# A zero product ahead of runs of three-pass products in a two-block transformer kernel

## The reference

```python
x = first_block(x, ...)     # i = 0: attention with 8 heads; i = 1: pooling over 2, 4, 8, 16 tokens;
                            # after each  x + squared_relu_mlp(rms_norm(x), w_up, w_down), d_ff 4096
h = h + merged @ w_o        # second block: a state-space branch and a latent attention of 16 heads
                            # from one wide projection w_in, merged by two gates
h = h + memory_cross_attention(rms_norm_2(h), rms_norm_2(mem), w_xq, w_xkv, w_xo)
h = h + hierarchical_moe(rms_norm_2(h), ...)      # 32 experts, 2 per token
return rms_norm_2(h, norm_final)
```

## Time and profile before

| | |
|---|---|
| runs of the kernel, us | 1225.2 median (1223.16, 1225.2, 1232.94) |
| the profiled execution, us | 1225.7 |
| its span, first to last instruction, us | 1223.7 |
| PE busy, us (share), instructions | 1189.7 (97%), 8980 |
| PE weight loads busy, us (share) | 1000.8 (82%) |
| DVE busy, us (share) | 787.9 (64%) |
| ACT busy, us (share) | 608.5 (50%) |
| mean granted clock of TensorE | 0.997 |

### The profile page before, as it was taken

How to read it: one execution, slowest core, us unless ns; L and a number is a source line. 1 busy time by engine, 2 the same in 40 slices (tenths; PEclk the granted TensorE clock), 3 DMA queues, 4 the chain that set the end, 5 groups by cost and what they waited for, 6 DMA issues and landing times.

```text
span 1223.7 us, 22272 instructions
## 1 busy us (share of the span) xinstructions
PE 1189.7 (97%) x8980; PEld 1000.8 (82%) x8980; DVE 787.9 (64%) x1330; ACT 608.5 (50%) x990; POOL 97.3 (8%) x100
## 2 busy tenths in 40 slices
PE   9999999999999999899999998999999999999997
PEld 7979999999899999898999998899999853333332
DVE  6876655566755556899899979869745462321214
ACT  6765545454645454767655586765554421111112
POOL 0000200000200000000000030001100004233301
PEclk9999999999999999999999999999999999999999
DMA  9654556564465565455544274455552999999996
GB/s 310 199 176 135 184 195 189 192 203 138 150 196 188 191 204 177 129 169 172 158 152 139 79 241 172 138 173 164 181 167 92 395 351 413 418 412 412 412 419 240
DMA packets 158707, 269.99 MB, mean 221 GB/s; under 512 B 17402, under 2 KB 121823, under 8 KB 154526
## 3 DMA queue, kind: packets, MB, share of 16 engines
q1 hardware_dynamic: 147824, 260.53, 60.8%
q0 software_dynamic: 10432, 8.16, 2.3%
q10 hardware_dynamic: 366, 0.12, 0.0%
HBM read 287.89 MB, written 12.58 MB: 246 GB/s over the span
## 4 chain that ended last, share of the span: by engine, by line
PE 76%; DVE 16%; ACT 4%; issue 3%; another core or an unknown queue 0%; DVEq 0%; ACTq 0%
PE psum L896 17%; PE psum L898 17%; PE psum L897 17%; PE psum L1509 11%; PE psum L1535 5%; DVE weights_parts L2196 4%; DVE arena L2599 3%; ACT weights_parts L1606 1%; PE psum L1469 1%; DVE smax L2320 1%; PE psum L1403 1%; PE psum L1520 1%; PE psum L1412 1%; DVE arena L2701 1%; DVE arena L2313 1%
## 5 line engine op out<-in xcount | busy, mean ns | idle before, releaser
L2196 DVE TENSOR_TENSOR weights_parts<-ring,weights_parts 128x1024 fp32r<-128x1024 f32 (+3 forms) x312 | 363.3, 1184 | 139.0 <-ACT weights_parts L1606 138.7
L1606 ACT ACTIVATE weights_parts<-ring 128x1024 fp32r<-128x1024 f32 (+3 forms) x312 | 309.4, 1011 | 149.0 <-PE psum L898 148.5
L896 PE MATMUL psum<-xnorm_parts,weights_parts 128*128 128x256 f32 x852 | 243.1, 285 | 6.6 <-DVE arena L2599 2.5
L897 PE MATMUL psum<-xnorm_parts,weights_parts 128*128 128x256 f32 x852 | 237.4, 279 | 0.0
L898 PE MATMUL psum<-xnorm_parts,weights_parts 128*128 128x256 f32 x852 | 237.4, 279 | 0.0
L896 PE MATMUL psum<-expert_cols,weights_parts 128*128 128x256 f32 (+1 forms) x688 | 193.1, 281 | 3.4 <-DVE expert_cols L2214 2.1
L897 PE MATMUL psum<-expert_cols,weights_parts 128*128 128x256 f32 (+1 forms) x688 | 190.7, 277 | 0.0
L898 PE MATMUL psum<-expert_cols,weights_parts 128*128 128x256 f32 (+1 forms) x688 | 190.7, 277 | 0.0
L896 PE MATMUL psum<-hidden_parts,weights_parts 128*128 128x256 f32 x640 | 179.3, 280 | 3.0 <-DVE hidden_parts L2667 1.7
L897 PE MATMUL psum<-hidden_parts,weights_parts 128*128 128x256 f32 x640 | 177.8, 278 | 0.0
L898 PE MATMUL psum<-hidden_parts,weights_parts 128*128 128x256 f32 x640 | 177.8, 278 | 0.0
(11 more groups left out here) (464 smaller groups left out, 1702.8 us busy)
## 6 DMA issues: line engine op xcount, KB each, us to landing
ring<-in_mlp_w_up SPq DMA_DIRECT2D x32, 1024.0 KB, 5.4
ring<-in_mlp_w_down SPq DMA_DIRECT2D x32, 1024.0 KB, 4.9
ring<-in_w_in SPq DMA_DIRECT2D x30, 1024.0 KB, 5.2
ring<-in_attn_w_qkv SPq DMA_DIRECT2D x12, 1024.0 KB, 6.2
expert_raw<-in_w_exp_gate SPq DMA_DIRECT2D x22, 512.0 KB
expert_raw<-in_w_exp_up SPq DMA_DIRECT2D x22, 512.0 KB
ring<-in_w_exp_down SPq DMA_DIRECT2D x11, 1024.0 KB
expert_raw<-in_w_exp_down SPq DMA_DIRECT2D x9, 1024.0 KB
```

What stands on the lines that cost most here:

```text
L896: pe.matmul(out, lh, rh, start=start, stop=False, **more)
L897: pe.matmul(out, lh, rl, start=False, stop=False, **more)
L1606: ins = act.activation(high, src, ACT.Copy)
L2196: ins = dve.tensor_tensor(low, src, high.bitcast(F32), ALU.subtract)
```

## The change

A helper `zero_product(b, start)` issues one bf16 product of the zero tile with itself, 128 by 128 stationary, 512 columns moving, into bank b. It is called behind the wait for the first half's low part and ahead of the first three-pass product. In `project_split` it opens the bank (start=True), and the chunk's own first product opens its columns again; in `add_down` it adds zeros to bank 4 (start=False). No value of the output changes. The flag is set for: qk 2; wo1 2; down 0 in the MLP's loop, in each of its three turns; up 13; "small" 1; xbc 1 and 5; the first gate chunk of groups 1 to 3; the second gate chunk of group 0; qb 0; mout 1; wo2 1. Over one execution that makes 20 products.

```diff
--- before.py
+++ after.py
@@ -903,10 +903,16 @@
                 pe.wait_ge(s["lo_ready"], shift + (2 * n + half + 1))
                 return high, low
 
-            def project_split(n, b, xn_from=None, shift=0, parts=(xh, xl), head_of=None):
+            def zero_product(b, start):
+
+                pe.matmul(bank(b)[:, 0:512], zeros[:, 0:P], zeros[:, 0:512], start=start, stop=False, skip_group_check=True)
+
+            def project_split(n, b, xn_from=None, shift=0, parts=(xh, xl), head_of=None, zero_first=False):
 
                 for m in range(2):
                     high, low = split_half(n, m, shift)
+                    if zero_first and m == 0:
+                        zero_product(b, True)
                     width = high.shape[2]
                     for k in range(KT):
                         if xn_from is not None and m == 0:
@@ -996,14 +1002,15 @@
                 stage = f"mlp{i}"
                 u, first = FILL[stage, "first"]
 
-                def up(it, n, xn_from=None):
+                def up(it, n, xn_from=None, zero_first=False):
                     b = n % 2
                     pe.wait_ge(made[b], it * 2 + (u[b] + n // 2))
-                    project_split(first + (2 * n - 1 if n else 0), b, xn_from, shift=it * 16, parts=PARTS[2 * i + 1])
-
-                def down(it, n, last=False):
+                    project_split(first + (2 * n - 1 if n else 0), b, xn_from, shift=it * 16, parts=PARTS[2 * i + 1],
+                                  zero_first=zero_first)
+
+                def down(it, n, last=False, zero_first=False):
                     pe.wait_ge(s["hid_ready"], it * 4 + (FC * i + n + 1))
-                    add_down(first + (2 * n + 2 if not last else 2 * n + 1), n % 2, it * 16, last)
+                    add_down(first + (2 * n + 2 if not last else 2 * n + 1), n % 2, it * 16, last, zero_first)
 
                 up(0, 0, XN_NO[2 * i + 1])
                 for b in range(4):
@@ -1012,10 +1019,10 @@
                 with pe.Fori(0, 3) as it:
                     for n in range(1, 5):
                         up(it, n)
-                        down(it, n - 1)
+                        down(it, n - 1, zero_first=(n == 1))
                 folded_sum(2 * i + 1, sq_late)
                 for n in range(13, FC):
-                    up(0, n)
+                    up(0, n, zero_first=(n == 13))
                     down(0, n - 1)
                 down(0, FC - 1, last=True)
 
@@ -1025,12 +1032,14 @@
                 for b in range(4, 8):
                     pe.matmul(bank(b), zeros[:, 0:P], zeros[:, :], start=True, stop=False, skip_group_check=True)
 
-            def add_down(n, buf, shift, last):
+            def add_down(n, buf, shift, last, zero_first=False):
 
                 hh = hid_h[:, buf, :].rearrange("p (k t) -> p k t", k=2)
                 hl = hid_l[:, buf, :].rearrange("p (k t) -> p k t", k=2)
                 for half in range(2):
                     high, low = split_half(n, half, shift)
+                    if zero_first and half == 0:
+                        zero_product(4, False)
                     for mm_ in range(4):
                         m = 4 * half + mm_
                         cc = slice(mm_ * P, (mm_ + 1) * P)
@@ -1071,7 +1080,7 @@
                 if j < 2:
                     project_high_first(j, open_bank("qk", j), j == 0)
                 else:
-                    project_split(j, open_bank("qk", j))
+                    project_split(j, open_bank("qk", j), zero_first=(j == 2))
                 if j == 1:
                     root_row()
                     pe.wait_ge(s["more_rows_in"], 16 * (len(ROWS_A) - 1 + len(ROWS_B)))
@@ -1117,7 +1126,7 @@
             wo1_part(0, [KT - 2, KT - 1])
             wo1_part(1, list(range(KT // 2, KT)))
             for j in (2, 3):
-                project_split(c.ordinal["wo1", j], open_bank("wo1", j))
+                project_split(c.ordinal["wo1", j], open_bank("wo1", j), zero_first=(j == 2))
             mlp(0)
 
 
@@ -1175,10 +1184,11 @@
                     total.then_inc(full[sums_bank], 1)
                 mm.then_inc(s["units_done"], 1)
             for j in (1, 2):
-                project_split(c.ordinal["win", j], open_bank("small", j), parts=PARTS["raw"])
+                project_split(c.ordinal["win", j], open_bank("small", j), parts=PARTS["raw"], zero_first=(j == 1))
 
             for j in range(12):
-                project_split(c.ordinal["win", 4 + j], open_bank("xbc", j), XN_NO[5] if j == 0 else None)
+                project_split(c.ordinal["win", 4 + j], open_bank("xbc", j), XN_NO[5] if j == 0 else None,
+                              zero_first=(j in (1, 5)))
                 if j == 4:
                     norm_sum(6)
                     norm_sum(7, sq[:, 3:5, :])
@@ -1190,8 +1200,8 @@
             def z_chunk(j):
                 project_split(c.ordinal["win", 16 + j], open_bank("z", j))
 
-            def gate_chunk(j):
-                project_split(c.ordinal["win", 24 + j], open_bank("gates", j))
+            def gate_chunk(j, zero_first=False):
+                project_split(c.ordinal["win", 24 + j], open_bank("gates", j), zero_first=zero_first)
 
             for g in range(NG):
                 def decays(q):
@@ -1248,11 +1258,11 @@
                     turn_inputs()
                     z_chunk(2 * g + 1)
                     state()
-                    gate_chunk(2 * g)
+                    gate_chunk(2 * g, zero_first=True)
                     b = open_bank("norm", 9 + g)
                     pe.wait_ge(s["gated_folded"], 2 * g)
                     pe.matmul(bank(b)[:, 0:TOK], ones, sq[:, 0, :], start=True, stop=True).then_inc(full[b], 1)
-                gate_chunk(2 * g + 1)
+                gate_chunk(2 * g + 1, zero_first=(g == 0))
                 wait_made("state", g)
                 pe.wait_ge(s["cs_ready"], g + 1)
                 wait_made("xsn", g, 0)
@@ -1303,6 +1313,8 @@
                     return mm
 
                 pe.wait_ge(s["lo_ready"], 2 * n + 1)
+                if j == 0:
+                    zero_product(b, True)
                 no_rope(0)
                 pe.wait_ge(s["lo_ready"], 2 * n + 2)
                 high, low = turned_columns(n)
@@ -1357,7 +1369,8 @@
             pe.wait_ge(s["kpe_copied"], 16)
             attention(LATENT, scores2, values2, CAUSAL, ssd_out)
             for j in range(4):
-                project_split(c.ordinal["mout", j], open_bank("mout", j), head_of=None if j else lambda k: H1 + 2 * k)
+                project_split(c.ordinal["mout", j], open_bank("mout", j), head_of=None if j else lambda k: H1 + 2 * k,
+                              zero_first=(j == 1))
                 if j == 0:
                     pe.wait_ge(s["mem_in"], 16)
                     for i in range(4):
@@ -1369,7 +1382,7 @@
                         mm.then_inc(full[b], 1)
             for j in range(4):
                 project_split(c.ordinal["wo2", j], open_bank("wo2", j), XN_NO["merged"] if j == 0 else None,
-                              parts=PARTS["merged"])
+                              parts=PARTS["merged"], zero_first=(j == 1))
                 if j == 0:
                     folded_sum(8, sq)
 
```

## The result

The changed kernel takes 1236.07 us (median of 12 runs, 1233.51 to 1238.35). The kernel before, run beside it and counted with its first three runs, takes 1229.33 us (12 runs, 1223.16 to 1233.22). The medians lie 6.7 us apart; the ratio on record, which is not the quotient of the medians, is 1.0045, 95% interval 1.0024 to 1.0065, or 5.5 us. So the changed kernel is slower by about half a per cent, where I had forecast 0.6 us less. Two things moved. The change costs some 6 to 7 us, and the kernel before is about 4 us slower than its first three runs said. Both come from the pace of the two MLP loops, as the experiments show.

A forecast was written before the change was run, and what follows sets the result against it. PE's distance between three-pass product starts, fast or slow, was taken to bound the kernel; +0.83 us of terms less 1.50 for pace kept across sums gave about -0.7, so 1224.6 us from a 1225.2 median, range 1221 to 1231.

The forecast's parts named there:

- Two paces, 113 and 118 ns, set where a run begins: Three-pass products on PE start at a fast or slow distance, some 4.45 ns apart, seemingly fixed where a run begins.
- After zero products comes the fast pace: Claimed from three cases: both MLPs behind clear_sums' four zero products, and the first chunk behind seven more.
- The MLPs' term, +1.92 us: Both MLPs, fast already: eight zero products at 0.24 us each on PE's path, nothing gained.
- the rival given 0.07 for both MLPs: Zero products inside both MLPs leave the slow pace behind them: 16 us more, 1236 to 1241 us, chance 0.07.
- wo1 -0.25, the gates +0.02, qb -0.02: Net us in wo1, gates of groups 1 to 3, and qb: 0.22 price per zero product against slow products turned fast.
- the case of a kept pace: If fast pace survives fp32 sums, second chunks gain too: gates 0.63, qb 0.23, wo2 0.64, together 1.50 us.
- qk, "small", xbc at 0: DVE sets the time there and PE's waits cover the price: 0, or +0.24 us each for five if cover is gone.
- wo2 -0.84, and -0.64 behind the sum: wo2, all PE: 238 slow products turn fast, -0.84 us; another 143 behind the fp32 sum, -0.64 if pace is kept.
- Fp32 sums mostly keep the pace, 9 of 12: Pace before and after fp32 sums counted the same in 9 of 12, so the kept total, -0.7 us, was taken.
- The profiled execution as the kernel's level: Profiled execution, 1225.7 us, expected to go to 1225.0; it stood 0.5 above the median of 1225.2.
- the second rival: Zero products inside MLPs leave slow pace: both MLPs 1236 to 1241 us, chance 0.07; one, about 1230, chance 0.06.
- The rule for the length of a product: The skill's columns / 2.4 + 2.5 ns gives 215.8 for zero products; by it the sum would be price only.

The follow-up runs named there:

- e6: Kernel before plus one bf16 zero product ahead of each of the 8 chunks in the MLPs' loops, each of another width (512 to 128 columns); one run, 1240.63 us.
- e10: Kernel before plus loop zero products, 512 columns at every other chunk and 64, 128, 192, 256 or 384 between, entered slow; one run, 1240.96 us.
- e12: Kernel before plus loop zero products, 512 columns at every other chunk and 272, 288, 320, 496, 504, 509 or 510 between; one run, 1246.18 us.
- e7: Kernel before with various openings ahead of the loops' 8 chunks: bf16 512-column and fp32 256-column zero products, singly or in groups; one run, 1253.56 us.
- e9: Kernel before with two 512-column zero products each time at down 0 in the MLPs' loops; 1228.53 us, ratio 0.9996.
- e2: Kernel before with only the zero products in the MLPs' loops (6 in one execution); 1238.01 us, ratio 1.0066.
- e8: Changed kernel with zero products of 256 columns in place of 512, at all 20 places; 1226.43 us, ratio 0.9981 to the kernel before.
- e1: Changed kernel without the 6 zero products in the MLPs' loops, the other 14 kept; 1227.33 us, ratio 0.9992 to the kernel before.
- e3: Kernel before with zero products only right behind fp32 sums of squares (up 13 in both MLPs, xbc 5, wo2 1); 1230.43 us, ratio 1.0005.
- e5: Zero products only behind fp32 sums, plus one fp32 zero-tile product ahead of the last zero product of clear_sums; 1227.91 us, ratio 0.9984.

## Why the prediction was wrong, point by point

- **Two paces, 113 and 118 ns, set where a run begins.** Right, and the base of everything measured since; but the pace can also change inside a row, with no opening and no wait, as at 888.4 us in the kernel before.
- **"After zero products comes the fast pace", three of three.** This is the step that failed. The three were groups of four and of seven, none a single product behind a three-pass one; and between the seven and the eight products timed behind them stand idle and 24 products of the first chunk (from 10.43 us on), so that case said little of zero products. One of 512 columns there is followed by the slow pace in 46 of 46 cases (e6, e10, e12), two by the fast one (e7, e9). And four are no proof either: entered slow they come out slow in 5 of 8. I carried a result across to another count, in a table of three.
- **The MLPs' term, +1.92 us, "with nothing gained".** The price was right: 0.23 us for one product of 512 columns in the trace after, 0.22 to 0.25 stated. The term missed that a single product would end the pace it found. The stretches measured +9.6 us in the profiled pair, about 8 x 0.23 = 1.8 of it price and the rest pace. That was the rival given 0.07 for both MLPs. Its mechanism and place are those of e2 and of the changed kernel, except that bank 4 and the hidden activations have no part in it: up positions answer like down ones. Its size is not: it added 16 us to 1225.2, while the medians differ by 6.7. In the profiled pair some 1,920 MLP products turned slow and not 2,860, because MLP 1's first turn stayed fast and up 13 and what follows came out fast behind their own zero products. That 1236.07 lies inside its 1236 to 1241 is owed to a kernel before that is 4 us slower than its three runs said.
- **wo1 -0.25, the gates +0.02, qb -0.02.** All stayed slow, so these were price only; the gates' second chunks, behind an fp32 sum, went fast, which I had only for the case of a kept pace. The stretch up to the loop cost 0.27.
- **qk, "small", xbc at 0.** Right: from the second MLP to wo2 1 the sum is -0.28 us. The cover was even larger than counted: behind its zero product the 312 products of qk turned from fast to slow, 1.4 us more of them, and still their weight loads end at 61.88 us, against 61.93 before. Where PE waits for DVE, the pace costs nothing.
- **wo2 -0.84, and -0.64 behind the sum.** Right in kind: -1.04 and fast products after 880 us. But in size it was luck. In the changed kernel's trace the three-pass products ahead of wo2 1's sum are fast already, so the zero product had nothing to turn there; the unchanged kernel in its second profile and e2 and e9 ran these chunks fast without one.
- **Fp32 sums mostly keep the pace, 9 of 12.** For the sums of `folded_sum`, which stand in a row without idle, this held better than I had claimed. In all 14 traces there are 40 with no zero product behind them: fast stayed fast 26 of 26 times, slow stayed slow 12 of 14 times. With a zero product behind the sum the pace was fast 16 of 16 times, 5 of them entered slow. So behind such a sum the zero product does what I had expected of it everywhere (behind the fp32 products of the zero tile in e7 it does not: entered fast, slow 6 of 6). The gates' sum (L1254) is no such case: in the changed kernel slow became fast across it in all three groups.
- **The profiled execution as the kernel's level.** Its 1225.7 us, and the first three runs' median, were good draws; over 12 runs the median is 1229.33. The range of three runs, 1223 to 1233, already said so. I read the highest one as noise and not as two slow loops (2 x 5.2 us), although the second rival's arithmetic priced just that. This moved the level and not the failed step: from 1229.33 the same sum gives 1228.7, and 1236.07 was measured.
- **The rule for the length of a product.** The zero products' starts are 216 ns apart in the trace after as before. The Trainium skill ("TensorE: Matmul & The Clock Gate", Back-to-back issue gap) gives 215.8 for such products taken alone, and by it the change would be price only; what made it dearer, the two paces, the page does not have. For a stream of weight loads and products the same section says about 131 ns at 512 columns, which the 216 ns here do not bear out.

## What to carry to other kernels

Before a stretch of hundreds of equal TensorE instructions is called fast, take the distance between their starts in more than one execution: the same program can run it at two paces, and the spread of its runs is then this lot being drawn. An opening put ahead of such a stretch in a loop makes one draw into all; whether it is the good one depends on its exact length and on what stands before it, so try several lengths and judge by the pace behind it and the width of the spread, not by its own price. And evidence from a group of four says nothing for one.

## What the runs showed of the hardware

- The pace of a row of fp32r products (weights 128 by 128, 256 columns) is either 113.3 or 117.8 ns at a granted clock of 1.00. It lasts for 1,100 products and through the turns of a loop. It changes behind products of another length and behind waits, but not only there: where the row goes over, without a gap, from a value chunk of xkv (activations stationary) to xq 0 (weights stationary), it went from slow to fast in the trace before (888.4 us) and from fast to slow in the trace after (896.4 us).
- Behind one bf16 product between them the pace goes by its number of columns: 64, 128, 192 and 254 to 256 fast, the ten widths tried from 272 to 504 slow (entered slow only), 508 slow, 509 and 510 fast, 511 and 512 slow, the same answer in every turn. That a single column decides (510 against 511) suggests a phase between weight loads and products. That is a guess: no run here shows such a phase, nor what it would be counted in.
- With a 512-column product between, the load behind it starts 5 to 6 ns after the zero tile's when a three-pass product stands before, and 216 ns after it when the sum of squares of `folded_sum` does, with 256 columns (e8) as with 512. Of the zero products behind sums of squares, the four places in each of the changed kernel, e1, e3, e5 and e8 came out fast, 20 of 20. Behind other fp32 products, in the gates and mout, they came out slow with few exceptions; why was not tried.
